# Taps 4 to 7 of seven convolution chunks moved from TensorE to GpSimd, in a fused kernel of two model blocks

## What is computed

```python
h = x @ pw1_w + pw1_b                 # 1024 -> 2048
a, g = split(h, 2)
h = a * sigmoid(g)
h = causal_dwconv(h, dw_w, dw_b)      # depthwise, 31 taps over the tokens
h = silu(layer_norm(h, ln_g, ln_b))
mix = h @ pw2_w + pw2_b
```

## Time and profile before

| | us |
|---|---|
| median of 3 runs | 1749.47 (1749.18 to 1750.5) |
| the profiled execution | 1748.82 |
| its span, first to last instruction | 1747.0 |
| TensorE (PE) busy | 1737.3 (99%) |
| VectorE (DVE) busy | 1063.2 (61%) |
| ScalarE (ACT) busy | 847.0 (48%) |
| GpSimd (POOL) busy | 18.4 (1%) |

### The profile page before, as it was taken

One profiled execution on the slowest core, in us unless ns is written; L12 is line 12 of the kernel. 1 busy time (PEld: TensorE's weight loads), 2 busy tenths in 40 slices (PEclk: granted clock), 3 DMA queues, 4 the chain that ended last, 5 costly groups with the idle time before them and its releaser, 6 DMA issues.

```text
span 1747.0 us, 22538 instructions
## 1 busy us (share of the span) xinstructions
PE 1737.3 (99%) x9213; PEld 1409.8 (81%) x9213; DVE 1063.2 (61%) x1666; ACT 847.0 (48%) x1330; POOL 18.4 (1%) x21
## 2 busy tenths in 40 slices
PE   9999999999999999999999999999999999999999
PEld 7887988888888897777778888888898866778766
DVE  6788864444433465777784444443378866656674
ACT  7789643333332355666463333342255455534542
POOL 0000100000000000000200000000000000000000
PEclk9999999999999999999999999999999999999999
DMA  5331233322222222111132232223213221122111
GB/s 216 110 121 49 85 109 97 96 97 97 96 97 96 101 81 73 51 59 49 61 114 93 97 98 97 98 91 109 97 61 106 97 70 63 61 97 97 61 60 49
DMA packets 44679, 155.43 MB, mean 89 GB/s; under 512 B 5281, under 2 KB 5537, under 8 KB 44577
## 3 DMA queue, kind: packets, MB, share of 16 engines
q1 hardware_dynamic: 44576, 153.99, 26.1%
HBM read 149.78 MB, written 2.10 MB: 87 GB/s over the span
## 4 chain that ended last, share of the span: by engine, by line
PE 92%; DVE 4%; ACT 2%; issue 1%; DMA 0%; SPq 0%; DVEq 0%; ACTq 0%
PE bank L553 92%; ACT tmp L1316 1%; DVE tmp L1990 1%; PE bank L1261 0%; DVE sbl L1999 0%; DVE wl L1999 0%; DVE XL L1999 0%; DMA wraw<-in_wstream 0%; ACT taps L1316 0%; DVE acc_q L1987 0%; ACT wh L1316 0%; DVE HL L1999 0%; DVE sbh L2455 0%; DVE X L1987 0%; ACT XH L1316 0%
## 5 line engine op out<-in xcount | busy, mean ns | idle before, releaser
L553 PE MATMUL bank<-XH,wh 128*128 128x512 f32 (+1 forms) x1504 | 583.4, 388 | 3.2 <-DVE XL L1999 0.7
L553 PE MATMUL bank<-XH,wl 128*128 128x512 f32 (+1 forms) x1504 | 573.5, 382 | 0.0
L553 PE MATMUL bank<-XL,wh 128*128 128x512 f32 (+1 forms) x1504 | 573.5, 382 | 0.0
L1999 DVE TENSOR_TENSOR wl<-wraw,wh 128x1024 fp32r<-128x1024 f32 (+1 forms) x264 | 319.6, 1219 | 238.2 <-ACT wh L1316 237.6
L1316 ACT ACTIVATE wh<-wraw 128x1024 fp32r<-128x1024 f32 (+1 forms) x264 | 276.2, 1052 | 250.3 <-PE bank L553 243.7
L553 PEld LDWEIGHTS bank<-XH,wh 128*128 128x128 f32 x1504 | 282.8, 188 | 68.5 <-issue 8.9
L553 PEld LDWEIGHTS bank<-XH,wl 128*128 128x128 f32 x1504 | 282.8, 188 | 55.3
L553 PEld LDWEIGHTS bank<-XL,wh 128*128 128x128 f32 x1504 | 283.1, 188 | 52.3 <-issue 0.7
L1987 DVE SCALAR_TENSOR_TENSOR tmp<-bank,prm,tmp 128x511 f32<-128x511 f32 x88 | 65.9, 749 | 172.1 <-ACT tmp L1316 170.6
L553 PE MATMUL bank<-HH,wh 128*128 128x512 f32 (+1 forms) x420 | 155.8, 371 | 0.0
L553 PE MATMUL bank<-HH,wl 128*128 128x512 f32 (+1 forms) x420 | 154.1, 367 | 0.0
(11 more groups left out here) (350 smaller groups left out, 2181.9 us busy)
## 6 DMA issues: line engine op xcount, KB each, us to landing
wraw<-in_wstream SPq DMA_DIRECT2D x276, 512.0 KB, 3.5
out<-X SPq DMA_DIRECT2D x8, 256.0 KB, 2.2
X<-in_xt SPq DMA_DIRECT2D x3, 512.0 KB, 8.5
pts<-in_pt SPq DMA_DIRECT2D x4, 256.0 KB, 4.1
eb<-lab SPq DMA_DIRECT2D x16, 64.0 KB, 2.0
cst<-in_consts SPq DMA_DIRECT2D x1, 810.5 KB, 9.9
X<-in_xt SPq DMA_DIRECT2D x2, 256.0 KB, 3.8
wraw<-in_wstream SPq DMA_DIRECT2D x2, 256.0 KB, 4.5
```

The costliest lines, as they stand in the source:

```text
L553: return pe.e.matmul(o, l, r, start=start, stop=stop, skip_group_check=True)
L1999: return dve.e.tensor_tensor(o, x, h.bitcast(F32), ALU.subtract)
```

## The change

For chunks 0 to 6 the block of taps 4 to 7, `("dw", 1, f)`, leaves TensorE and the weight stream; a hole takes its place, so the units and their transfers stay as they are. GpSimd makes these four taps: for each one product `taps_p = cin * weight`, the weight column spread over 512 tokens with step 0, and one add into `Y`; after each product it waits for itself. For chunk 7 TensorE keeps all seven blocks, and GpSimd makes taps 2 and 3, which VectorE made. `first_taps(f)` for the other chunks waits for all GpSimd sums of its chunk and is issued one step later, right ahead of `conv_sum(f)`. The parameter array grows by 32 columns for the weights of the taps.

Since `("dw", 2, f)` stands second in its unit, the `feed` of the tap unit no longer prepares anything: the unit three ahead is prepared by the first `feed` of the next step. In the attention, `more_pairs` leaves out its first `feed_group` on VectorE; the next one makes two remainders.

```diff
-    o.extend([("dw", n, 0) for n in range(1, 8)] + [None])
+    o.extend([None] + [("dw", n, 0) for n in range(2, 8)] + [None])
...
-    o = [("b1", 16), ("dwb", 8), ("dwt", 24), ("lng", 8), ("lnb", 8), ("b2", 8)]
+    o = [("b1", 16), ("dwb", 8), ("dwt", 56), ("lng", 8), ("lnb", 8), ("b2", 8)]
...
# tensor_program, taps(f)
-        for n in range(1, 8):
+        first = 2 if f < 7 else 1
+        for n in range(first, 8):
...
# scalar_program and vector_program, step f
         if 0 < f < 7:
-            feed(("dw", 1, f - 1))
+            feed(("dw", 2, f - 1))
...
# vector_program, conv_sum(f)
-        dve.wait_ge(dve.own, tapped[f])
+        if f < 7:
+            dve.wait_ge(dve.own, tapped[f])
+        else:
+            dve.wait_ge(s.pool, pool_taps(8))
...
# vector_program, first_taps(f)
         dve.wait_ge(s.c_base, f + 1)
+        dve.wait_ge(s.pool, pool_taps(f + 1))
...
# vector_program, step f
-        first_taps(f)
         if 2 <= f < 7:
             conv_stats(f - 2)
+        if f:
+            first_taps(f - 1)
...
# vector_program, more_pairs
-                        feed_group(mat, range(KD), [c])
+                        if n > 1:
+                            feed_group(mat, range(KD), [c])
...
# gpsimd_program
+def pool_taps(f):
+    return 8 * f if f < 8 else 60
...
+    for f in range(8):
+        y, ci = m.Y[:, f, :], m.cin[f % 2]
+        pool.wait_ge(s.c_base, f + 1)
+        for k in range(4, 8) if f < 7 else range(2, 4):
+            u = m.taps_p[k % 2][:, :]
+            n = pool.mark(tt(u, ci[:, k:S + k], P("dwt", 7 * f + k - 1).broadcast_to([128, S]), ALU.mult))
+            pool.wait_ge(pool.own, n)
+            pool.mark(tt(y, y, u, ALU.add))
```

More of the change, by code:

```diff
@@ L57, in weight_order @@
     o.extend(("pw1", k, c) for f in range(2) for k in range(4, KD) for c in (f, 8 + f))
-    o.extend([("dw", n, 0) for n in range(1, 8)] + [None])
+    o.extend([None] + [("dw", n, 0) for n in range(2, 8)] + [None])
     for f in range(2, 7):
         o.extend([("pw1", k, f) for k in range(KD)] + [("pw1", k, 8 + f) for k in range(KD)])
-        o.extend([("dw", n, f - 1) for n in range(1, 8)] + [None])
+        o.extend([None] + [("dw", n, f - 1) for n in range(2, 8)] + [None])
     o.extend([("pw1", k, 7) for k in range(KD)] + [("pw1", k, 15) for k in range(KD)])
-    for f in (6, 7):
-        o.extend([("dw", n, f) for n in range(1, 8)] + [None])
+    o.extend([None] + [("dw", n, 6) for n in range(2, 8)] + [None])
+    o.extend([("dw", n, 7) for n in range(1, 8)] + [None])
     o += grouped("pp0", 2, list(range(8)), 1)
@@ L151, in __init__ @@
                 self.spare[self.at[mat, 2 + 2 * e, 0] // NU] = (layer, e)
-        for e, key in enumerate((("dw", 1, 6), ("dw", 1, 7), ("pp0", 0, 4), ("pw2", 0, 0))):
+        for e, key in enumerate((("dw", 2, 6), ("dw", 2, 7), ("pp0", 0, 4), ("pw2", 0, 0))):
             self.spare[self.at[key] // NU] = (2, e)
@@ L383, in place @@
         m.cinl = ring(ph, "cinl", 2, [128, PAD + S], FR)
+        sb(ph, "conv_units", [128, 15 * S - 6 * (PAD + S + 1)])
+        m.taps_p = [sb(ph, "taps_p0", [128, S])]
+        sb(ph, "conv_emb", [128, 2 * S])
+        m.taps_p.append(sb(ph, "taps_p1", [128, S]))
     m.PP, m.HH, m.HL, m.pts = [], [], [], []
@@ L761, in taps @@
                 r = slice(32 * i, 32 * i + 32)
-                mm(bank[b + i][:, :], h[r, cols], ch[r, tok], n == 1, False)
+                mm(bank[b + i][:, :], h[r, cols], ch[r, tok], n == first, False)
             for i in range(4):
@@ L1500, in scalar_program @@
         fn(m.cinh[f % 2][:, :], m.cin[f % 2][:, :], ACT.Copy).then_inc(s.c_hi, 1)
-        fn(m.Y[:, f, :], m.cin[f % 2][:, 1:S + 1], ACT.Identity, scale=P("dwt", 3 * f), bias=P("dwb", f)).then_inc(s.c_base, 1)
+        fn(m.Y[:, f, :], m.cin[f % 2][:, 1:S + 1], ACT.Identity, scale=P("dwt", 7 * f), bias=P("dwb", f)).then_inc(s.c_base, 1)
         if f == 4:
@@ L2238, in first_taps @@
         dve.wait_ge(s.c_base, f + 1)
-        n2 = dve.mark(stt(y, ci[:, 2:S + 2], P("dwt", 3 * f + 1), y, ALU.mult, ALU.add))
+        dve.wait_ge(s.pool, pool_taps(f + 1))
+        n2 = dve.mark(stt(y, ci[:, 2:S + 2], P("dwt", 7 * f + 1), y, ALU.mult, ALU.add))
         dve.wait_ge(dve.own, n2)
-        tapped.append(dve.mark(stt(y, ci[:, 3:S + 3], P("dwt", 3 * f + 2), y, ALU.mult, ALU.add)))
+        tapped.append(dve.mark(stt(y, ci[:, 3:S + 3], P("dwt", 7 * f + 2), y, ALU.mult, ALU.add)))
     def conv_stats(c):
@@ L2918, in vector_program @@
                     input_low(c - 1)
+def pool_taps(f):
+    return 8 * f if f < 8 else 60
 def gpsimd_program(pool, m, s):
-    C = m.C
+    C, P = m.C, m.P
     def tt(o, i0, i1, op):
         return pool.e.tensor_tensor(o, i0, i1, op)
+    for f in range(8):
[6 more added lines that the diff above has]
+            pool.mark(tt(y, y, u, ALU.add))
     def add_sum(i, c, x0, x):
@@ L3026, in lay_out @@
     put("dwb", f["a_dw_b"][0])
-    put("dwt", np.ascontiguousarray(taps[1:4].reshape(3, 8, 128).transpose(1, 0, 2)))
+    put("dwt", np.ascontiguousarray(taps[1:8].reshape(7, 8, 128).transpose(1, 0, 2)))
     put("lng", f["a_ln_g"][0])
```

## The result

The changed kernel took 1772.70 us (median of 4 runs, 1772.03 to 1773.24), the kernel before beside it 1749.33 (4 runs, 1748.96 to 1750.5): ratio 1.0132, interval 1.0119 to 1.0145, slower by 23.4 us. The forecast was 1780.7 in a range of 1758 to 1791. Direction and mechanism held; 8 us of the 31.3 forecast did not come. The profiled execution took 1773.24, its span is 1771.5.

The account below looks back on a forecast made before the run. TensorE, busy 99% of the span, was taken to bound the kernel. Terms +8.1, +14.6, +6.2, +2.9 and -0.5 sum to +31.3, so 1748.8 becomes 1780.1, forecast as a median of 1780.7; range 1758 to 1791 us.

Parts of the forecast that it names:

- mechanism: Convolution: VectorE ops with two SBUF inputs and GpSimd ops exclude each other, +1.10 us per held op; TensorE waits.
- The rival without a mutual hold: Convolution: GpSimd and VectorE do not hold each other; 1748.8 us, no change; chance 8%.
- The rival in which only the lock's own time counts: Convolution: waits fall into gaps, a step takes 16.8 us; +10.9, 1760 us; chance 15%.
- The faster rival: Chunk 0's GpSimd sums end before delaying anything, TensorE stays the bound; -4.6, 1744.9 us; chance 6%.
- the price of an op of GpSimd: Each GpSimd tap op in the convolution takes 1.30 us, with a gap of 0.15.
- the price of a hold: Full convolution step: six GpSimd ops hold VectorE at 1.10 us each, 6.6 us together.
- +8.1: Chunk 0: GpSimd's sums end late and VectorE is held, so taps(1) starts at 52.5 instead of 44.44 us.
- The lower bound's product of 1.0: Lower bound, 1766 us: GpSimd ops with a step-0 column take 1.0 us each, some 15 us less over seven steps.
- a full step: Convolution: VectorE's 13.2 plus 6.6 of holds make 19.8 us instead of 16.16; four steps, +14.6 us.
- Step 6: taps(5) to taps(6): three more remainders with holds, 6.7, less 4.2 of wait; 22.3 instead of 16.1 us, +6.2.
- The tail: After taps(6): VectorE's ops before chunk 7's base start ScalarE's copies about 8 us after taps(6), not 5.1; +2.9.
- The attention: Remainder ahead of `OL` taken out, TensorE's wait of 0.47 us there goes; -0.5 us.
- that 5% and over 1791: Rival on the clock: idle TensorE's granted clock falls to 1.2 of 2.4 GHz for a part; over 1790 us; 5%.

Follow-up runs that it names:

- the load alone: Kernel before plus as many GpSimd ops of the same kind on buffers of their own, awaited only by the last sum: 1774.62 us, ratio 1.0142.
- Moving the roundings: Changed kernel with ScalarE's spare roundings of step 6 issued behind `cinh` and the base instead of ahead: 1770.51 us, ratio 1.012.

## Why the prediction was right, and where its size was off

**The mechanism** held: VectorE's taps became up to 1.8 us long and its `Y<-Y,tmp` adds up to 1.6, though most stayed below the 1.8 forecast; bank adds are unchanged; TensorE waits for `wl` ahead of taps(1), taps(3) and taps(4), for `Y` ahead of taps(6). The rival without a mutual hold (1748.8) is refuted by the load alone, which costs 25 us though nobody waits for it, and with it what the Trainium skill's Mode Summary ("Advanced Engine Details and Errata", VectorE Performance Modes) would have made of the time. The rival in which only the lock's own time counts (1760) is refuted by the same run: VectorE's ops are held inside their rows, and that becomes the step. The faster rival (1744.9) needed chunk 0 done in 8.6 us; GpSimd took 10.7 (28.87 to 39.60). Its gain was not there to be had either: with GpSimd's work left out the kernel saves 1.6 us, not 4.6, and the trace shows only 0.7 of it in the convolution, since ScalarE and VectorE bound its end. Of the five steps two, from taps(1) and from taps(4), end without the wait that was foretold: TensorE, at a lower clock, was itself late (busy 18.17 of 18.20 us in the first of them, last section).

**The terms that were mis-sized are the price of an op of GpSimd and, with it, the price of a hold.** The prediction took 1.30 us and a gap of 0.15 for all eight ops of a chunk, and six holds of 1.10 in each step. Six ops are held in a step, as counted; the prices are lower. Measured:
- A product with a step-0 column takes 1.04 us alone (79.86), an add 1.29 (80.97), and the gap is 0.08 (80.89 to 80.97). In chunk 0 this is most of the difference: GpSimd needs 10.7 us, not 12.4, so VectorE's taps start 9.9 us after taps(0) instead of 11.4, and from there to taps(1) the 12.4 measured stand against 12.8. Hence +6.2 for +8.1. The lower bound's product of 1.0 was right, but for half of the ops only.
- In a full step the six ops that are held lose 4.5 us together, not 6.6: each waits for what is left of an op of GpSimd, 0.4 to 0.9 us. GpSimd begins at ScalarE's base, when the three remainders are done, and 11.8 us later it is through. 13.2 + 4.5 = 17.7 is near the mean of 72.66 / 4 = 18.2; forecast was 19.8. Over four steps that is the other 6.6 us. Of the +8.0 that did come there, up to 2.5 are not holds but the lower clock, by the estimate in the last section; the prediction's sum had no term for it.

**Step 6** was right in size (+6.2) and half right in its reasons. The three remainders ahead of the bank adds took 6.6 us, as worked out (6.7). But the prediction had VectorE waiting 0.7 us for `cinh` there, and it waits 4.64, for a transfer that ScalarE's queue passes on to it (2.21 before, in the same step: 110.76 to 112.97); this adds 3.9 us that the sum did not have. That the step still came out at the forecast size is luck in part: the cheaper holds and the dearer wait cancelled. Moving the roundings is worth 2.2 us by the medians, 1.2 of it in this step.

**The tail** came as worked out, +3.2 for +2.9: ScalarE's first copy of chunk 6 starts at 155.19, 8.0 us after taps(6), where it started 5.1 after the earlier trace rows. **The attention** gave its 0.5, by the traces alone: the wait of the earlier trace rows is gone in the changed kernel too.

**Where the time went**, from the experiments: the edits outside GpSimd -1.6 (no GpSimd work; not clear of nothing); GpSimd's part +24.8 (1772.70 - 1747.92), of which 7.7 hang on chunk 0. The savings of the single experiments can't be added up, since most of them shorten the same waits of TensorE for VectorE.

Open is how much exactly the lower clock cost, for which there is only the estimate below, and whether a form that multiplies and adds in one GpSimd op would do better; no run tries either.

## What to carry to other kernels

Work given to GpSimd is priced by what VectorE does at that time: in these runs each of its ops that reads two operands from SBUF paid mostly 0.4 to 1.1 us beside GpSimd ops of 1.04 and 1.29 us that read SBUF, while ops with one operand in a PSUM bank, and all ops beside memsets, went free. An engine that is only 77% busy (12.44 of 16.20 us) can still become the bound: with 0.7 us of waiting VectorE had about 3.0 us to spare in a step, which is four holds of the measured mean of 0.75 us (an estimate), and it got six. Its lead carried two chunks of them and no more. So find out first what the idea is worth when the helper is free (here 1.6 us, not clear of nothing), and take only as many pieces as the slack covers.

## What was not expected of the hardware

**The granted clock.** Stretches of the changed kernel between the starts of the taps, in the columns of the earlier trace rows:

```profile
29.80:52.10 22.30, 15.55 (x121) 12.53 (x121) 15.12 (x14) 12.78 (x19) 20.48 (x16) 0.90 0.08 25
52.10:70.30 18.20, 18.17 (x120) 14.77 (x120) 14.33 (x16) 11.92 (x18) 10.79 (x8) 0.84 0.26 89
70.30:87.20 16.90, 15.55 (x121) 12.58 (x120) 15.70 (x17) 13.30 (x20) 11.52 (x8) 1.00 0.27 92
```

It was 1.00 in both stretches of the earlier trace rows, and 1.000 on average over the kernel before. After the idle 6.78 us the products start 0.43 us apart (52.69, 53.12), at 1.2 GHz, instead of 0.23 (70.64, 70.87), at 2.4. I had given that 5% and over 1791; it came, and the time stayed below.

What it cost is seen where the chain in order of time runs through TensorE at that clock (start, us, what):

```profile
52.13 7.15 PE bank L557 x72
59.30 0.59 ACT tmp L1321
...
66.68 1.36 DVE Y L1995
```

The 72 instructions of taps(1) carry the chain for 7.15 us; those of taps(2), at 1.00, take 4.5 (70.31 to ScalarE's first copy at 74.78). ScalarE had idled 2.47 us when its copies could begin at 59.30, and VectorE's last add of the chunk waited for the last of them. So the lower clock cost up to 2.5 us in this step: an estimate from these rows, since no run has the waits without it. Behind taps(4) and taps(6), which also began at the lower clock, the chain does not run through TensorE, and no cost is seen. That VectorE bounds the step all by itself is seen with chunk 0 on TensorE: at a clock of 1.00 a step takes 17.9 us there as well (98.73 to 116.64).

**GpSimd's form matters**: 1.04 us for 128x512 with a step-0 column as second operand, 1.29 with two full ones, 0.53 for a memset (63.2 us for 120). **Cost of being held is mutual**: the same two ops take 1.48 and 1.62 beside VectorE, so a chunk on GpSimd takes 11.8 us (73.58 to 85.42) instead of the 9.9 that its own lengths and gaps make.
